# Eight transformer stages on one core: modulation pieces moved between stages, a new opening, forget gates by heads

## The chip, the cores and the metric

One core of one Trainium2 chip runs the whole program. The metric is the time of one execution on the device in microseconds, the median of three runs. Nothing is shared with another core; all tensors come from the chip's memory (HBM) and all are 32-bit floats.

## What is computed

256 tokens of width 1024 go through eight stages, in this order (the names are the kernel's): `moba` (attention of 8 heads, a pooled branch and two gates), `conv` (a gated feed-forward with a causal convolution of width 3), `ffn`, `swa` (attention of 16 query heads over a window), `ffn`, `ffn`, `fox` (attention of 16 heads with forget gates), `ffn`. Each stage is normalised, shifted and scaled, and added back through a gate:

```python
c_act = jax.nn.silu(c)
mod = c_act @ ada_w[l] + ada_b[l]          # (B, 6D) in the first block, (B, 9D) a layer in the second
h = rms_norm(x, norm_g) * (1 + scale) + shift
x = x + gate * mixer(h)                    # or 0.5 * gate * swiglu(h, w13, w2)

def swiglu(h, w13, w2):
    gate, up = jnp.split(h @ w13, 2, axis=-1)
    return (jax.nn.silu(gate) * up) @ w2

def fox_mixer(...):
    q, k, v, fl = jnp.split(h @ w_in, [HD, 2 * HD, 3 * HD], axis=-1)   # fl: one column a head, 16 in all
    log_f = jax.nn.log_sigmoid(fl + b_f)
    F = jnp.transpose(jnp.cumsum(log_f, axis=1), (0, 2, 1))            # over the 256 tokens
    s = q @ k.T + Fq[..., None] - F[:, :, None, :]
```

D is 1024, the hidden width of the feed-forwards 2816. `mod` holds shift, scale and gate of every stage: 6144 + 2 x 9216 columns, each a product of 1024 rows, which makes 48 chunks of 512 columns.

## The kernel before, in words

**Weight units.** Every weight matrix is cut into units of 128 x 2048 numbers (1 MB): 24 for `moba`, 33 for `conv` and each `ffn` (eleven steps `j` over 256 hidden columns, two units of the up projections and one of the down projection each, in the order `FFN_ORDER`), 10 for `swa`, 16 for `fox`. `W0[s]` is the first unit of stage `s`. The products keep 32-bit precision in three passes: a unit is split into a high part, `hi` (ACT, L504), and the rest, `lo` (DVE, `split_to`, L926), and so are the activations (`h_hi` and `h_lo`, `o_hi` and `o_lo`); PE does hi x hi, lo x hi and hi x lo into the same bank (lines in threes, such as L1411 to L1413 and L1374 to L1376). Raw units go through five slots that SP fills; slot w is free once PE is through with unit w - 5. `hi` and `lo` are double buffered. Each engine has its own list of work, written out by hand, and takes it strictly in order. `take(w)` on PE does what the schedule hangs onto unit w, and then waits for its `lo`.

**Modulation.** Four chunks of the 48 are done in the opening (`PRO_CHUNKS`), the others during the stages before the one that needs them: `CHUNKS_IN[s]` says how many in each. A chunk is four pieces of 256 rows by 512 columns (512 KB), loaded by POOL (L461) into the two halves of `ada`. Piece n can be loaded only when piece n - 2 has been used up. DVE adds a piece to one of two accumulators `ada_sum` in two steps (`ada_op`, L885 for a chunk's first step, L888 for the others), each a multiplication by the condition's column. When a chunk has its eight steps, PE sums it over the partitions (`sums`, L1342: four products of one column, eight records in the trace), DVE adds the bias (`columns`, L910) and for a gate's chunks PE turns the columns into rows (`gate_rows`, L1354). The first step of chunk c waits for the sums of chunk c - 2. `PIECES_AT`, `SUMS_AT`, `COLS_AT` and `GATES_AT` say behind or ahead of which unit each part stands. On DVE, the pieces of unit w come right after `lo` of unit w; on PE the sums of unit w come before its products.

The schedule of a `conv` or `ffn` stage before the change, for n0 chunks:

```python
at = [3 + (p0 * 27 // (4 * n0) if n0 > 4 else p0) for p0 in range(4 * n0)]
```

In the third stage (nine chunks) that is 36 pieces on units 3 to 29 with one or two each. In `swa`, unit 4 has two pieces and attention steps 8 to 15 one each; its three sums stand in step 1 and at its last units.

**Opening.** SP loads `c`, then five pieces of 512 rows by 512 columns (1 MB, rows of 2 KB), `x`, and three more pieces. DVE adds each with four steps of 512 columns (`pro_piece`), and PE sums each chunk as soon as it is there: two before the bias tables, two after the transposes of `x`. Then DVE makes `lo` of unit 0 and splits `h`.

**A stage's start.** `turn_x` on PE (L1362) turns the normalised `work` of 128 tokens (half t = 0 or 1), ACT applies shift and scale (L544), DVE splits (`split_h`, L961 and L963). DVE's `boundary` has the order: root of half 0, `lo` of unit 1, split of half 0, residual of half 1, `lo` of unit 2, root of half 1, `lo` of unit 3, split of half 1. ACT's has hi of unit 3 before `normed` of half 1 (L532).

**First stage's end.** DVE merges the two branches in four parts (semaphore `merged`), PE waits for all four, then `out_units` does four units for t = 0 and t = 1, with the gate rows due at the first.

**Forget gates.** 48 products (L1305 to L1307) with h as the weights and `f_hi` or `f_lo` of 16 columns moving give 128 tokens x 16 heads, twice. DVE adds the bias (L1263), ACT and DVE make log sigmoid, and PE adds up over the tokens with a triangular matrix (L1797 to L1799). Each token row is then 16 heads wide; `f_parts` holds the result by heads.

## Time and profile before

| what | value |
|---|---|
| three runs | 1540.94, 1527.5, 1535.44 us; median 1535.44 |
| the profiled execution | 1542.21 us, of which the span on the engines is 1540.4 |
| PE busy | 1454.9 us, 94% of the span |
| DVE, ACT, POOL busy | 1055.7 (69%), 732.5 (48%), 140.4 (9%) |
| mean granted clock of TensorE | 0.967 |
| moved by DMA | 333.94 MB, 217 GB/s on average |

The span is what the timeline shows; the profiled execution's time has 1.8 us around it and lies 0.4% above the median. PE's records overlap: a product's record is longer than the distance to the next, so its busy time is read as coverage, and the distance between starts is what a product costs.

### The profile page before, as it was taken

Reading aid. Unit: us, or ns where it says so; the run is one execution under the profiler, and the core shown is the slowest. Engines: PE = TensorE matmul, PEld = TensorE weight load, DVE = VectorE, ACT = ScalarE, POOL = GpSimd, SP = SyncE. Lnnn points to the kernel's source line nnn. Section 1 sums busy time; section 2 is a strip of 40 time slices with the busy share of each in tenths; the row PEclk is TensorE's granted clock in tenths of the full one; section 3 lists DMA queues with packets and bytes.
Section 4 is the critical chain, followed back from the end, with each engine's and each line's share of the span. In section 5 each row is a group of like instructions: output and inputs, shape, how many; then the busy total and the mean of one; then the engine's idle time right before and its main releaser. Section 6 shows DMA issues by size and latency. Waiting matters only on the chain.

```text
span 1540.4 us, 18813 instructions
## 1 busy us (share of the span) xinstructions
PE 1454.9 (94%) x7463; PEld 1208.0 (78%) x7463; DVE 1055.7 (69%) x1498; ACT 732.5 (48%) x1036; POOL 140.4 (9%) x199
## 2 busy tenths in 40 slices
PE   3799988999999999988999999999999899999998
PEld 2688978999978888765688878788877776688886
DVE  5768866988977777667577777776767346466444
ACT  2554445444564433765544335633337466554432
POOL 1011100110001111000011110011110100000000
PEclk9999999999999999985999999999999799999999
DMA  9677664777759888361478886788863442376552
GB/s 322 236 227 244 233 220 163 267 252 242 250 180 313 284 284 301 113 218 55 156 244 299 289 265 221 235 300 291 288 224 117 133 144 75 105 239 201 170 189 81
DMA packets 192395, 333.94 MB, mean 217 GB/s; under 512 B 8834, under 2 KB 132494, under 8 KB 192308
## 3 DMA queue, kind: packets, MB, share of 16 engines
q1 hardware_dynamic: 164464, 236.02, 45.6%
q0 software_dynamic: 27264, 96.49, 19.6%
q8 instruction: 60, 0.98, 0.3%
q10 hardware_dynamic: 580, 0.23, 0.1%
q14 instruction: 27, 0.22, 0.0%
HBM read 331.55 MB, written 1.15 MB: 216 GB/s over the span
## 4 chain that ended last, share of the span: by engine, by line
PE 67%; DVE 8%; ACT 5%; issue 3%; DMA 2%; ACTq 0%; DVEq 0%
PE bank L1411 9%; PE bank L1413 9%; PE bank L1412 9%; PE bank L1374 7%; PE bank L1376 6%; PE bank L1375 6%; DVE lo L926 3%; PE bank L1305 2%; PE bank L1307 2%; PE bank L1306 2%; PE bank L1539 2%; DMA ada<-in_ada_w 2%; DVE ada_sum L888 2%; PE bank L1342 2%; PE bank L1540 2%
## 5 line engine op out<-in xcount | busy, mean ns | idle before, releaser
L926 DVE TENSOR_TENSOR lo<-raw,hi 128x2048 fp32r<-128x2048 f32 x215 | 490.8, 2286 | 88.0 <-ACT hi L504 87.3
L504 ACT ACTIVATE hi<-raw 128x2048 fp32r<-128x2048 f32 x215 | 405.4, 1909 | 34.4 <-DMA raw<-in_w_out 13.9
L1411 PE MATMUL bank<-hi,h_hi 128*128 128x512 f32 x704 | 279.3, 397 | 2.6 <-DVE lo L926 1.8
L888 DVE SCALAR_TENSOR_TENSOR ada_sum<-ada,c_act,ada_sum 128x512 f32<-128x512 f32 x312 | 234.1, 750 | 65.2 <-DMA ada<-in_ada_w 56.7
L1413 PE MATMUL bank<-hi,h_lo 128*128 128x512 f32 x704 | 275.4, 391 | 0.0
L1412 PE MATMUL bank<-lo,h_hi 128*128 128x512 f32 x704 | 275.2, 391 | 0.0
L461 POOL DMA_DIRECT2D ada<-in_ada_w x176 | 125.3, 712 | 1105.8 <-DVE ada_sum L888 1090.4
L1374 PE MATMUL bank<-hi,o_hi 128*128 128x512 f32 x504 | 205.5, 408 | 8.6 <-DVE lo L926 7.6
L1376 PE MATMUL bank<-hi,o_lo 128*128 128x512 f32 x504 | 197.9, 393 | 0.0
L1375 PE MATMUL bank<-lo,o_hi 128*128 128x512 f32 x504 | 197.5, 392 | 0.0
L611 ACT ACTIVATE KT<-bank 128x256 f32<-128x256 f32 x88 | 33.8, 384 | 322.7 <-PE bank L1413 322.6
L1411 PEld LDWEIGHTS bank<-hi,h_hi 128*128 128x128 f32 x704 | 133.0, 189 | 32.6 <-DVE lo L926 3.5
L1413 PEld LDWEIGHTS bank<-hi,h_lo 128*128 128x128 f32 x704 | 132.8, 189 | 28.6
L1412 PEld LDWEIGHTS bank<-lo,h_hi 128*128 128x128 f32 x704 | 133.0, 189 | 26.5
L1305 PE MATMUL bank<-h_hi,hi 128*128 128x256 f32 x480 | 139.0, 290 | 1.0 <-DVE lo L926 1.0
L1306 PE MATMUL bank<-h_lo,hi 128*128 128x256 f32 x480 | 136.7, 285 | 0.0
L1307 PE MATMUL bank<-h_hi,lo 128*128 128x256 f32 x480 | 136.7, 285 | 0.0
L1374 PEld LDWEIGHTS bank<-hi,o_hi 128*128 128x128 f32 x504 | 95.4, 189 | 31.2 <-DVE lo L926 10.6
L1376 PEld LDWEIGHTS bank<-hi,o_lo 128*128 128x128 f32 x504 | 95.2, 189 | 21.2
L1375 PEld LDWEIGHTS bank<-lo,o_hi 128*128 128x128 f32 x504 | 95.7, 190 | 17.4
L1305 PEld LDWEIGHTS bank<-h_hi,hi 128*128 128x128 f32 x480 | 93.0, 194 | 3.0 <-issue 2.5
L1306 PEld LDWEIGHTS bank<-h_lo,hi 128*128 128x128 f32 x480 | 93.1, 194 | 0.2
(206 smaller groups left out, 1875.3 us busy)
## 6 DMA issues: line engine op xcount, KB each, us to landing
ada<-in_ada_w POOLq DMA_DIRECT2D x176, 512.0 KB, 5.3
raw<-in_ffn_w SPq DMA_DIRECT2D x176, 512.0 KB, 5.4
raw<-in_ffn_w SPq DMA_DIRECT2D x44, 1024.0 KB, 6.3
raw<-in_w_up SPq DMA_DIRECT2D x22, 1024.0 KB, 5.1
raw<-in_w_in SPq DMA_DIRECT2D x16, 1024.0 KB, 7.4
raw<-in_fox_w_in SPq DMA_DIRECT2D x12, 1024.0 KB, 5.1
raw<-in_w_down SPq DMA_DIRECT2D x11, 1024.0 KB, 5.2
raw<-in_swa_w_in SPq DMA_DIRECT2D x6, 1024.0 KB, 5.2
```

Of the source, the lines that this page charges most:

```text
L504: nc.scalar.activation(hi[:, n % NS, :], raw[:, n % NS, :], ACT.Copy).then_inc(hi_ready, 1)
L888: nc.vector.scalar_tensor_tensor(acc, in0=src, scalar=c_act[:, col:col + 1], in1=acc, op0=ALU.mult, op1=ALU.add).then_inc(ada_step, 1)
L926: nc.vector.tensor_tensor(lo[:, n % NS, :], raw[:, n % NS, :], hi[:, n % NS, :].bitcast(F32), ALU.subtract).then_inc(lo_ready, 1)
L1305: mm(outp, wh, xh, start=start, stop=False, skip_group_check=True)
L1306: mm(outp, wh, xl, start=False, stop=False, skip_group_check=True)
L1307: return mm(outp, wl, xh, start=False, stop=stop, skip_group_check=True)
L1374: mm(outp, xk_hi, wh[:, k, cut], start=start, stop=False, skip_group_check=True)
L1375: mm(outp, xk_hi, wl[:, k, cut], start=False, stop=False, skip_group_check=True)
L1376: ins = mm(outp, xk_lo, wh[:, k, cut], start=False, stop=stop, skip_group_check=True)
L1411: mm(bank[:, :], xk_hi, wh[:, i, :], start=k == 0, stop=False, skip_group_check=True)
L1412: mm(bank[:, :], xk_hi, wl[:, i, :], start=False, stop=False, skip_group_check=True)
L1413: ins = mm(bank[:, :], xk_lo, wh[:, i, :], start=False, stop=k == KD - 1, skip_group_check=True)
```

## The change

1. `CHUNKS_IN` goes from 6, 6, 9, 3, 9, 9, 0, 2 to 6, 7, 11, 0, 9, 9, 0, 2. `swa` (the fourth stage) has no pieces and sums any more. With more than ten chunks the schedule begins at unit 2, and a piece whose accumulator isn't free yet is put no earlier than the unit of that sum. In the third stage this gives, for units 2 to 27, the piece counts 2 2 2 1 2 2 1 2 2 0 3 1 2 2 2 2 1 2 2 1 2 0 3 1 3 1, with sums at units 5, 8, 12, 14, 16, 18, 20, 24, 26, 28 and 30.
2. Opening pieces are 128 rows by 2048 columns (rows of 8 KB), one step of 2048 columns each into one accumulator `pro_sum`; `x` is loaded fourth. All 16 sums of one column come after the last piece.
3. Forget gates: `f_hi` and `f_lo` are the weights, h moves (24 products of 256 columns), so that the result has a head in each row; DVE adds up over the tokens with a scan, and PE has no part in that.
4. First stage: columns a unit earlier; `out_units` waits for two merged parts before units 0 and 1 and for four before 2 and 3, and takes unit and gate rows first.
5. Start of `conv`: root and `normed` of half 1 come before `lo` of unit 2 and hi of unit 3, and PE turns half 1 only after both first units of half 0.

```diff
-CHUNKS_IN = [6, 6, 9, 3, 9, 9, 0, 2]
+CHUNKS_IN = [6, 7, 11, 0, 9, 9, 0, 2]
...
-        at = [3 + (p0 * 27 // (4 * n0) if n0 > 4 else p0) for p0 in range(4 * n0)]
-        for u0 in at:
-            PIECES_AT[w0 + u0] = PIECES_AT.get(w0 + u0, 0) + 1
+        from0, over = (2, 26) if n0 > 10 else (3, 27)
         turns, at_sums = [], []
-        for u1 in (at[4 * c0 + 3] + 2 for c0 in range(n0)):
+        for c0 in range(n0):
+            for p0 in range(4 * c0, 4 * c0 + 4):
+                u0 = from0 + (p0 * over // (4 * n0) if n0 > 4 else p0)
+                if c0 > 1:
+                    u0 = max(u0, at_sums[c0 - 2])
+                PIECES_AT[w0 + u0] = PIECES_AT.get(w0 + u0, 0) + 1
+            u1 = u0 + 2
...
-        COLS_AT.update({w0 + u: 1 for u in (11, 13, 15, 18, 20, 23)})
+        COLS_AT.update({w0 + u: 1 for u in (10, 12, 14, 17, 19, 22)})
...
-    elif kind0 == "swa":
-        PIECES_AT[w0 + 4] = 2
...
-            for i in range(8):
-                if i == 5:
+            for i in range(KD):
+                if i == 3:
                     sp.dma_start(x[:, :, :], a["x"][0].rearrange("(t p) d -> p t d", p=P)).then_inc(x_full, 16)
-                sp.dma_start(pro[i], ada_columns(i // 2)[:, 4 * (i % 2):4 * (i % 2) + 4, :]).then_inc(pro_full[i], 16)
+                sp.dma_start(pro[i], a["ada_w"][0][P * i:P * (i + 1), 0:2 * D]).then_inc(pro_full[i], 16)
...
                 split_to(W0[b] + 2)
                 norm_stats(b, 1)
-                split_to(W0[b] + 3)
-                normed(b, 1)
+                if KINDS[b] == "conv":
+                    normed(b, 1)
+                    split_to(W0[b] + 3)
+                else:
+                    split_to(W0[b] + 3)
+                    normed(b, 1)
...
             def pro_piece(i):
                 dve.wait_ge(pro_full[i], 16)
-                for k in range(4):
-                    ada_op(i // 2, 4 * (i % 2) + k, pro[i][:, k, :])
+                if i == 0:
+                    nc.vector.tensor_scalar(pro_sum[:, :], pro[i], c_act[:, 0:1], None, ALU.mult).then_inc(pro_step, 1)
+                else:
+                    dve.wait_ge(pro_step, i)
+                    nc.vector.scalar_tensor_tensor(pro_sum[:, :], in0=pro[i], scalar=c_act[:, i:i + 1],
+                                                   in1=pro_sum[:, :], op0=ALU.mult, op1=ALU.add).then_inc(pro_step, 1)
...
+                    nc.vector.tensor_tensor_scan(fz[:, 5, :], ones[0:16, 0:1].to_broadcast([16, T]), fz[:, 4, :], 0.0,
+                                                 ALU.mult, ALU.add).then_inc(cum_done, 1)
                     block_sums(s, 3)
                     block_norm(s, 3)
...
-                        if u:
-                            turn_x(s, 1)
+                    elif u == 0:
+                        turn_x(s, 1)
...
                 for o, t in [(0, 0), (0, 1), (1, 0), (2, 0), (3, 0), (1, 1), (2, 1), (3, 1)]:
                     if t == 0:
                         take(first + o)
+                        pe.wait_ge(merged, 2 if o < 2 else 4)
                     elif o == 3:
                         turn_x(s + 1, 0)
+                    if o == 0:
+                        pe.wait_ge((merge_a, merge_b)[t], 4)
...
-            sums(1)
             turn_x(0, 0)
             turn_x(0, 1)
-            sums(2)
+            pe.wait_ge(pro_step, KD)
+            for i in range(2 * KD):
+                ins = mm(M[:, i:i + 1], pro_sum[:, P * i:P * (i + 1)], ones[:, 0:1], start=True, stop=True)
+            ins.then_inc(ada_used, PRO_CHUNKS)
...
-                    pe.wait_ge(merged, 4)
                     out_units(s, h_hi, h_lo)
...
-                    for t in range(2):
-                        for k in range(KD):
-                            ins = product(A[0][:, 16 * t:16 * (t + 1)], h_hi[:, k, P * t:P * (t + 1)],
-                                          h_lo[:, k, P * t:P * (t + 1)], f_hi[:, k, :], f_lo[:, k, :], k == 0, k == KD - 1)
+                    pe.wait_ge(h_ready, 4 * s + 4)
+                    held = lambda w, k: w[:, k:k + KD, :].rearrange("p a b -> p (a b)")
+                    for k in range(KD):
+                        ins = product(A[0][:, 0:T], held(f_hi, k), held(f_lo, k), h_hi[:, k, :], h_lo[:, k, :],
+                                      k == 0, k == KD - 1)
                     ins.then_inc(fl_done, 1)
...
-                    pe.wait_ge(lf_ready, 1)
-                    lf = fz[:, 4, :]
-                    mm(A[1][0:16, 0:P], lf[:, 0:16], tri, start=True, stop=True)
-                    mm(A[1][0:16, P:T], lf[:, 0:16], ones[:, :], start=True, stop=False)
-                    mm(A[1][0:16, P:T], lf[:, 16:32], tri, start=False, stop=True).then_inc(cum_done, 1)
```

The diff also takes the calls of `columns`, `pieces` and `sums` out of `attention_step`, `step` and the `swa` branch, moves two small tables to other buffers and their waits with them, and puts `f_parts` before `lo` of unit 6 in `fox`.

## Rows read from the trace of the kernel before

**Rows 1.** The page's busy shares and granted clock in 40 slices.

```profile
PE 1454.9 (94%) x7463; PEld 1208.0 (78%) x7463; DVE 1055.7 (69%) x1498; ACT 732.5 (48%) x1036; POOL 140.4 (9%) x199
...
PEclk9999999999999999985999999999999799999999
```

**Rows 2.** The view of waits, PE: what line waited for what; us, times, longest us.

```profile
PE bank L1702 <- DMA TB<-in_fox_k_g: 17.3, 1, 17.3
PE bank L1362 <- ACT work L532: 8.7, 2, 4.4
PE bank L1374 <- DVE lo L926: 7.6, 11, 1.6
...
PE bank L1342 <- DVE modc L910: 6.1, 2, 3.6
...
PE bank L1797 <- DVE fz L1269: 5.1, 1, 5.1
```

**Rows 3.** Timeline, first stage: start, us, engine line op [idle before, releaser].

```profile
149.30 1.84 PE L1342 MATMUL bank<-ones,ada_sum 128*128 128x1 f32 x8 [2.55 <-DVE modc L910]
...
202.38 4.49 DVE L926 TENSOR_TENSOR lo<-raw,hi 128x2048 fp32r<-128x2048 f32 x2
...
202.52 2.08 PE L1354 MATMUL bank<-kon,modc 128*128 128x128 f32 x8 [4.46 <-DVE h_lo L1149]
...
204.82 0.63 PE L1375 MATMUL bank<-lo,h_hi 128*128 128x512 f32 x1
...
211.13 0.95 PE L1342 MATMUL bank<-ones,ada_sum 128*128 128x1 f32 x8
```

**Rows 4.** Timeline, the sixth stage's gap of 1.79 us.

```profile
1138.43 1.47 PE L1342 MATMUL bank<-ones,ada_sum 128*128 128x1 f32 x8 [1.79 <-DVE KT L1009]
```

**Rows 5.** Timeline, opening.

```profile
37.35 3.11 DVE L888 SCALAR_TENSOR_TENSOR ada_sum<-ada,c_act,ada_sum 128x512 f32<-128x512 f32 x4
...
40.68 1.84 PE L1342 MATMUL bank<-ones,ada_sum 128*128 128x1 f32 x8 [3.59 <-DVE modc L910]
...
46.33 0.77 PE L1539 MATMUL bank<-hi,h_hi 128*128 128x512 f32 x1 [3.81 <-DVE h_lo L963]
```

**Rows 6.** Windows: us, busy of PE, PEld, DVE, ACT, POOL; PEclk, DMA share, GB/s.

```profile
38.00:40.00 2.00, 0.00 (x0) 0.00 (x0) 1.89 (x4) 1.76 (x1) 0.00 (x0) 1.00 1.05 392
674.00:724.00 50.00, 42.17 (x136) 24.68 (x135) 34.32 (x106) 35.15 (x84) 1.42 (x2) 0.58 0.22 70
```

**Rows 7.** Timeline, start of the conv stage.

```profile
234.12 1.89 ACT L504 ACTIVATE hi<-raw 128x2048 fp32r<-128x2048 f32 x1
...
236.77 1.94 PE L1362 MATMUL bank<-kon,work 128*128 128x128 f32 x8 [4.42 <-ACT work L532]
...
238.26 0.48 DVE L885 TENSOR_SCALAR ada_sum<-ada,c_act 128x512 f32<-128x512 f32 x1
```

**Rows 8.** Timeline, forget gates of the seventh stage.

```profile
1193.89 0.17 PE L1305 MATMUL bank<-f_hi,h_hi 128*128 128x16 f32 x1
...
1201.21 0.77 PE L1539 MATMUL bank<-hi,h_hi 128*128 128x512 f32 x1
...
1215.67 0.60 PE L1797 MATMUL bank<-kon,fz 128*16 128x128 f32 x2 [5.06 <-DVE fz L1269]
```

**Rows 9.** Timeline, second feed-forward (third stage), a sum and the pieces behind it.

```profile
526.85 0.49 DVE L885 TENSOR_SCALAR ada_sum<-ada,c_act 128x512 f32<-128x512 f32 x1 [4.32 <-PE bank L1342]
...
528.42 0.70 POOL L461 DMA_DIRECT2D ada<-in_ada_w  x1 [7.74 <-DVE ada_sum L888]
...
529.68 2.28 DVE L926 TENSOR_TENSOR lo<-raw,hi 128x2048 fp32r<-128x2048 f32 x1
...
532.19 0.39 PE L1374 MATMUL bank<-hi,o_hi 128*128 128x512 f32 x1
...
532.66 1.54 DVE L888 SCALAR_TENSOR_TENSOR ada_sum<-ada,c_act,ada_sum 128x512 f32<-128x512 f32 x2 [0.69 <-DMA ada<-in_ada_w]
```

**Rows 10.** Tile ada from 440 to 620 us: DMA landing times.

```profile
DMA to landing us min/median/max: 4.1/5.3/8.1
```

More of the change, by code:

```diff
@@ L839, in _ @@
                     act.wait_ge(f_exp, 1)
[L840 removed]
+                    nc.scalar.activation(fz[:, 3, :], fz[:, 2, :], ACT.Ln, bias=ones[0:16, 0:1]).then_inc(f_ln, 1)
                     block_evict(s, 1)
@@ L971, in boundary @@
                 residual(b - 1, 1)
-                split_to(W0[b] + 2)
-                root(b, 1)
+                if KINDS[b] == "conv":
+                    root(b, 1)
+                    split_to(W0[b] + 2)
+                else:
+                    split_to(W0[b] + 2)
+                    root(b, 1)
                 split_to(W0[b] + 3)
@@ L1092, in attention_step @@
                     out_lo(s, (t - 3) // 2)
-                columns(int(t in COLS_STEP[kind]))
-                pieces(int(t in PIECES_STEP[kind]))
             def step(ins):
@@ L1168, in _ @@
                                     ALU.mult).then_inc(cols_done, 1)
-            columns(1)
-            pro_piece(4)
-            columns(1)
+            for i in range(4, 6):
+                pro_piece(i)
             root(0, 0)
             root(0, 1)
-            for i in range(5, 8):
+            for i in range(6, KD):
                 pro_piece(i)
-            columns(2)
+            dve.wait_ge(ada_used, PRO_CHUNKS)
+            nc.vector.tensor_tensor(modc[:, 0, 0:2 * KD], M[:, 0:2 * KD], cols[:, C_ADAB:C_ADAB + 2 * KD],
+                                    ALU.add).then_inc(mod_ready, PRO_CHUNKS)
+            dve.wait_ge(mod_ready, PRO_CHUNKS)
+            nc.vector.scalar_tensor_tensor(acol[:, 0, :], in0=modc[:, 0, KD:2 * KD], scalar=1.0,
+                                           in1=cols[:, C_N1:C_N1 + KD], op0=ALU.add, op1=ALU.mult).then_inc(acol_ready, 2)
             split_to(0)
```

80 lines of the change are left out of this document (35 added, 45 removed).

## The prediction

> **What bounds the kernel now.** I read the page's head first: PE is busy for 1454.9 of 1540.4 us and its granted clock is full in all but two of the 40 slices [rows 1]. So an edit pays only if it takes PE work away, closes one of PE's gaps, or spares the slow records that follow a gap. Then the waits of PE, longest first [rows 2]: of 85.5 us idle, 17.3 lie in the opening, where PE waits for first data and the change alters nothing; 8.7 are two stage boundaries (L1362), 7.6 are eleven short waits for a weight unit's low half (L1374), 6.1 are two sums held up by `modc` (L1342), 5.1 the forget gates (L1797); a sixth, of 4.5, ends the first stage (L1354, [rows 3]). The change aims at the last five. Last I read the timeline around each place, asking of each which engine arrives last and what stands before it in its order.
>
> **Full and half clock.** A 512-column product reads 0.63 us at half clock (1.2 GHz) and starts 0.43 after the one before; at full clock (2.4 GHz) it reads 0.39 (the row stands with the second feed-forward's) and starts 0.228 apart. The eight records of one sum read 0.95 at full clock and 1.84 at half [rows 3]. After a gap of 4.46 us PE goes on at half: gate columns and 24 products take 211.13 − 202.52 = 8.6 us, where 1.0 + 24 × 0.228 = 6.5 would do. I take 2.4 us of slow records behind each long gap. A gap of 1.79 us was enough once [rows 4].
>
> **Opening, +3.** Now the last piece is added in four steps of 0.78, 37.35 to 40.46, the last sum runs from 40.68 at half clock for 1.84, and the first product starts at 46.33 [rows 5]. The new pieces carry the same bytes in longer rows. The queue is already at 392 GB/s with a DMA share above 1 [rows 6], so they land no earlier: the last at about 35.5. One step of 2048 columns is bounded by the 2048-column `lo` subtraction, 4.49 for two [rows 3], and four of 0.78; I take 2.35, so DVE ends at 37.9, 2.6 us sooner. But three of the four groups of sums now run earlier, in PE's idle time; after the change all sixteen follow the last piece: 32 records of 0.23 at half clock, 7.4 us against 1.84, or +5.5. Net +2.9. At full clock they would take 3.8 and the part would be −0.6; since PE has been idle, I take half. Range −3 to +5, the lower end for pieces landing sooner.
> The Trainium skill (DMA: Bandwidth & Descriptors, "Why small descriptors are slow") puts a fixed overhead of about three cycles on each packet: from 2 KB to 8 KB rows that would be an estimated 3% of the landing time, about 0.7 us; the share above 1 in the row shows no room for it.
>
> **First stage inside, −1.5.** The columns are taken a unit earlier, which ends the wait of 2.55 us at 149.30 [rows 3] and the slow records behind it. DVE and the landings stand close behind, so I count half of the gap's 2.55 plus a little. Range −3 to 0.
>
> **Its end, −6.** Before `out_units` PE waits for all four merged parts: 4.46 us, then the gate columns 2.08 instead of 0.95 to 1.05 and the slow products, 1.4. Under the change the gate columns and the first two units need less and come first; the fourth part is ready about 4.4 us after PE's last product, and PE reaches it some 10 us on. All of 4.46 + 1.0 + 1.4 = 6.9 could go; that DVE also owes two `lo` of 2.28 each from 202.38 keeps me at −6.2. Range −7 to −5.
>
> **Conv's start, +3.** PE waits 4.42 us to 236.77 for the second half's `work`, turns it in 1.94 and goes on with u1 of the first half [rows 7]. Under the change u1 comes first and fills 2.9 of the gap. But ACT now makes `work` before hi(27), which moves from 234.12 to about 236 and ends 237.7; its `lo` ends 240.0; then come two pieces (2.9 us) where there was one (1.25, from 238.26), before the second half of `h` is split. That half is ready at 243.9 to 245.1, not 242.0, PE idles some 7.6 us in front of it and then runs at half clock: its first two units end at about 251.6, not 248.5. Range 0 to +4. The seventh chunk adds +0.5 in the body (0 to +1).
>
> **Second attention, −4.** Twelve pieces and three sums leave. At 674 to 724 us PE is busy 42.17 of 50 at a granted clock of 0.58, DVE only 34.32 [rows 6]: the steps there are short dependent ones, and DVE is not what they lack. What goes is DVE time ahead of waits at the edges: −3.9 (−2 to −8). The three sums cost 3.16 here and 3 × 0.95 where they go: −0.3.
>
> **Forget gates, −12.** Now 48 narrow products take 7.3 us (27 at 0.11 apart, the rest at 0.21, for PE falls to half clock amid them), and the twelve products behind them 5.5 instead of 2.7; a gap of 5.06 ends at 1215.67; three cumulative products take 1.4; the 24 products behind take 7.5 instead of 5.5 [rows 8]. After: 24 products of 256 columns at 0.12 are 2.9 (−4.4), the next twelve at full clock (−2.7), two waits for ACT's evictions of 0.9 and 1.5 in place of the gap (−2.6), no cumulative products (−1.4), no slow ones (−2.0): −13.1. I keep −12, range −14 to −8: a wait of 1.5 may bring half clock back. The scan is not in the trace; 256 columns lie between a 128x32 operation (0.19) and a 512-column one (0.75), and it stands on DVE beside 5 us of PE work: nothing.
>
> **The second feed-forward, +27.** This decides. Two chunks more come in: eight pieces, and the new schedule puts three pieces into one unit twice (u12, u24) and again at u26 with a `hidden` step; now none has more than two. `ada` has two buffers, so the third piece's load is issued only when the first has been used. One such cycle is in the trace [rows 9]. PE's sum lets DVE go at X = 526.85; the first piece is used up at X + 1.2; POOL issues its successor at X + 1.57; it has landed when DVE takes it at X + 5.8, after the `lo` of the next unit, which ended at X + 5.1, with PE needing it at X + 5.34: 0.2 us of slack. In the new unit the third piece stands ahead of that `lo`: it ends at X + 5.8 + 1.54 = 7.3, `lo` at X + 9.6, and PE stands still for 4.3 us. The whole wait lies on PE's path, since everything else on DVE's order is as late. So 4.3 at u12, 4.3 at u24, 5.0 at u26, and 1.1 for the step that turns the hidden units right behind. The start of the stage has pieces from its second unit now: two of them (2.9 us) stand ahead of the second half's root, and PE, which has no gap there now, gets 3.7 and then 1.5 of slow records: +5.1. Behind the three long stalls I add 2.4 each, 7.2. Sum 4.3 + 4.3 + 5.0 + 1.1 + 5.1 + 7.2 = 27. The load in the cycle took 4.24 from issue to landing; the stage's median is 5.3 [rows 10], and with it the sum is 33. If instead DVE catches up by way of gaps that I don't see, little of it comes: +3.
> The Trainium skill (DMA: Bandwidth & Descriptors, "Anatomy of one DMA — SWDGE (gpsimd) path") gives about 2.0 us plus the bytes over 436 GB/s for such a load, an estimated 3.2 us for 512 KB; the rows here never go below 4.1. By the page each stall would be 1 us shorter and this part an estimated +24.
>
> **Sum.** +3 − 1.5 − 6.2 + 3.1 + 0.5 − 3.9 − 0.3 − 12 + 27 = +9.7. The profiled execution took 1542.21, 6.8 above the median of the runs, 1535.44; its sum is 1551.9, and on the median that is 1545.
>
> **Rivals.** A, the feed-forward hides it: DVE is busy about 70% overall, and if it runs further ahead of PE at u12 and u24 than the 0.2 us above, the stalls shrink to 5 us in all. Then the gains stand almost alone: 1535 − 22 + 8 = 1521. For it: eleven waits for `lo` sum to only 7.6 us. Against: they exist at all, and slack in the cycle shown is 0.2. B, slower than before: loads of `ada` land in 6 to 8 us, since more of them run beside the weights; the stage shows up to 8.1 and 16.1 us of DVE waiting for them already [rows 10]. Each triple unit then costs 5.5 to 7 and units with two pieces also run late, about twelve of them by 0.5 each: +40 in the stage, 1558. It decides from a median landing of about 6. C, the forget gates give 5 rather than 12, because ACT's evictions hold PE and the clock stays at half: 1552. That the second attention loses nothing when its pieces leave, since it never waited for DVE, would be +4, within the range.
>
> **Chances.** The forecast 0.45 (own range 1536 to 1556), A 0.22 (1512 to 1526), B 0.22 (1554 to 1566), C 0.11 (1548 to 1556). The range 1519 to 1561 leaves out some 0.1 on either side. One per cent, about what a measurement of this kernel can tell from no change, puts the bounds at 1520.1 and 1550.8: faster 0.12 from A and a little from the forecast's edge, 0.15; slower is a quarter of the forecast, nearly all of B and two thirds of C, 0.39; the rest 0.46.
>
> **What would show it.** Right: in the second feed-forward three PE waits for `lo` of over 3 us, each with DVE waiting for `ada` just before; a DVE with 32 sum records of 7.4 us before the first product; no wait at L1354 at the first stage's end; the forget part from its first product to the first logits shorter by 12 us. Wrong: PE idle time in the second feed-forward up by under 8 us, or half clock absent behind the stalls; then I have mis-sized how far DVE runs ahead, and the change is a gain.

## Result: slower by 2.75%, and the profile after

The changed kernel takes 1576.08 us (median of 4 runs, 1572.44 to 1578.78) against 1533.2 for the kernel before (4 runs). The ratio is 1.0275, with a 95% interval of 1.0223 to 1.0327. The prediction said 1545, range 1519 to 1561. The profiled execution took 1578.78, its span is 1577.0; the terms of the prediction are compared with it.

The page's head and clock row (the counterpart of [rows 1]):

```profile
PE 1454.8 (92%) x7433; PEld 1202.7 (76%) x7433; DVE 1052.6 (67%) x1473; ACT 731.9 (46%) x1036; POOL 139.8 (9%) x198
...
PEclk9999998999999999898699999999999989999999
```

PE is busy exactly as long as before, 1454.8 against 1454.9 us. So whatever work the forget gates took from it, slow records elsewhere took again; all 36.6 us that the span grew are idle time of PE: 122.2 instead of 85.5. The view of waits says behind what (PE; us in total, times, longest; the counterpart of [rows 2]):

```profile
PE bank L1720 <- DMA TB<-in_fox_k_g: 26.4, 1, 26.4
PE bank L1394 <- DVE lo L933: 16.3, 12, 4.0
PE bank L1442 <- DVE KT L1020: 10.4, 5, 3.0
PE bank L1382 <- ACT work L536: 10.0, 3, 6.3
PE bank L1431 <- DVE lo L933: 6.7, 7, 4.4
...
PE bank L1326 <- DVE h_lo L970: 5.6, 1, 5.6
PE bank L1362 <- DVE o_lo L1244: 5.4, 1, 5.4
PE bank L1431 <- DVE h_lo L970: 4.9, 3, 4.4
...
PE bank L1603 <- DMA f_rows<-forget_rows: 2.2, 1, 2.2
```

L1720 is the old L1702, L1394 the old L1374. The three waits at which the change aimed (old L1342, L1354, L1797) are gone. In their place stand a longer first one, waits for `lo` twice as long in sum (26.6 us on all lines against 13.4), two waits that were short before (L1442 for `KT`, 1.6 on the old L1422, and L1431 for `h_lo`, 0.8 on the old L1411), and three that the trace before didn't have at all (L1326, L1362, L1603).

From the timelines of all kernels I made one table, which the rest rests on: the time of PE's first product, and then the length of each stage, from the start of its first `turn_x` on PE to the next stage's (for the first stage, from that first product).

| kernel | first product | moba | conv | ffn (3rd) | swa | ffn (5th) | ffn (6th) | fox | ffn | span |
|---|---|---|---|---|---|---|---|---|---|---|
| before | 46.3 | 179.4 | 207.4 | 199.8 | 129.9 | 202.4 | 205.2 | 169.6 | 200.3 | 1540.4 |
| after | 52.8 | 182.1 | 212.8 | 242.2 | 124.9 | 200.1 | 202.0 | 159.8 | 200.4 | 1577.0 |
| e1_old_schedule | 50.2 | 181.1 | 209.2 | 202.2 | 128.8 | 199.9 | 203.3 | 158.2 | 200.3 | 1533.3 |
| e2_four_buffers | 50.4 | 180.8 | 213.3 | 211.9 | 122.6 | 200.0 | 200.6 | 161.4 | 200.3 | 1541.2 |
| e3_table_later | 53.1 | 175.5 | 212.3 | 238.7 | 122.5 | 199.9 | 200.1 | 161.4 | 200.3 | 1563.8 |
| e4_short_rows | 47.7 | 180.5 | 213.2 | 242.4 | 122.6 | 199.9 | 204.1 | 161.4 | 200.3 | 1572.2 |
| e5_paced | 50.7 | 181.1 | 212.8 | 239.9 | 124.5 | 200.8 | 200.7 | 157.9 | 200.3 | 1568.6 |
| e6_old_boundary | 52.7 | 175.6 | 209.2 | 238.7 | 122.5 | 199.9 | 200.0 | 161.4 | 200.3 | 1560.3 |
| e7_piece_later | 52.8 | 180.9 | 213.4 | 240.8 | 124.5 | 200.3 | 202.6 | 156.6 | 200.3 | 1572.3 |
| e8_together | 46.4 | 175.8 | 209.5 | 204.0 | 130.0 | 199.9 | 202.0 | 161.3 | 200.3 | 1529.1 |
| e9_even | 50.2 | 182.1 | 213.1 | 228.8 | 122.5 | 201.5 | 203.2 | 158.2 | 200.3 | 1560.0 |
| e10_best | 44.8 | 176.0 | 208.8 | 204.1 | 125.0 | 202.8 | 200.4 | 156.8 | 200.3 | 1519.0 |
| e11_chunks_alone | 46.0 | 179.7 | 208.8 | 238.3 | 125.0 | 205.0 | 202.5 | 162.8 | 200.4 | 1568.4 |
| e12_gates_alone | 44.5 | 178.5 | 207.0 | 200.0 | 127.2 | 199.8 | 201.3 | 161.2 | 200.3 | 1519.9 |

The fifth and sixth stages have the same instructions in all of these and still vary by 5 us, so a difference of a few us in one stage of one trace is no finding by itself. The last stage varies by no more than 0.1.

**The opening.** Timeline of the kernel after (the counterpart of [rows 5]):

```profile
29.76 0.48 PE L1720 MATMUL bank<-kon,TB 128*128 128x128 f32 x1 [26.39 <-DMA TB<-in_fox_k_g]
...
31.61 0.17 DVE L1183 TENSOR_SCALAR cols<-cols 128x3 f32<-128x3 f32 x1 [6.79 <-ACT cols L722]
31.69 2.35 DVE L1177 SCALAR_TENSOR_TENSOR pro_sum<-V,c_act,pro_sum 128x2048 f32<-128x2048 f32 x1
...
41.83 1.44 PE L1733 MATMUL bank<-ones,pro_sum 128*128 128x1 f32 x6 [0.63 <-DVE pro_sum L1177]
...
52.78 0.76 PE L1559 MATMUL bank<-hi,h_hi 128*128 128x512 f32 x1 [3.97 <-DVE h_lo L970]
```

The large step takes 2.35, as estimated. But the small rows of biases and gains arrive for PE's L1720 at 29.8, not 20.5, and on DVE a small step on `cols`, which needs them, stands ahead of the fifth piece: DVE idles 6.79 us, and then four steps follow, each 2.35. The sums can start at 41.83 where the prediction had 37.9.

**The first stage's end and conv's start:**

```profile
212.37 1.15 POOL L449 DMA_DIRECT2D TB<-bias_by_distance  x1 [25.82 <-DVE h_lo L1158]
...
228.54 1.91 ACT L508 ACTIVATE hi<-raw 128x2048 fp32r<-128x2048 f32 x1 [13.84 <-DMA raw<-in_w_up]
...
234.85 1.97 PE L1382 MATMUL bank<-kon,work 128*128 128x128 f32 x8 [6.26 <-ACT work L536]
...
253.67 0.58 PE L1326 MATMUL bank<-hi,h_hi 128*128 128x256 f32 x1 [5.57 <-DVE h_lo L970]
```

At the sum of unit 18 PE is 9.6 us later than before (195.10 against 185.50); at the sum of unit 21, inside `out_units`, it is only 2.75 later (213.88 against 211.13). So a gain of 6.9 us at `out_units` is real. Then ACT waits 13.84 us for conv's second unit. And at 253.67 is the wait that the prediction had put at 7.6 us.

**The third stage.** The cycle of [rows 9], now at u12, where three pieces meet:

```profile
536.58 0.49 DVE L892 TENSOR_SCALAR ada_sum<-ada,c_act 128x512 f32<-128x512 f32 x1 [4.34 <-PE bank L1362]
...
538.16 0.71 POOL L465 DMA_DIRECT2D ada<-in_ada_w  x1 [10.83 <-DVE ada_sum L895]
...
542.18 1.54 DVE L895 SCALAR_TENSOR_TENSOR ada_sum<-ada,c_act,ada_sum 128x512 f32<-128x512 f32 x2 [2.68 <-DMA ada<-in_ada_w]
...
543.63 2.29 DVE L933 TENSOR_TENSOR lo<-raw,hi 128x2048 fp32r<-128x2048 f32 x1
...
545.98 0.80 PE L1394 MATMUL bank<-hi,o_hi 128*128 128x512 f32 x1 [3.90 <-DVE lo L933]
```

With X = 536.58 the third piece starts at X + 5.6 and `lo` ends at X + 9.3; the prediction had 5.8 and 9.6. What it didn't have is in the tile's view of the whole stage (DVE's idle time ahead of pieces, by what ended it; then landing times; the counterpart of [rows 10]):

```profile
  DMA ada<-in_ada_w: 36.4, 21
...
DMA to landing us min/median/max: 3.9/5.2/7.5
```

DVE waited 16.1 us for pieces in this stage before, 11 times. It is 36.4 now, 21 times, with the same landing times. So loads are not slower. There are more of them than two buffers let through without waits, where they stand.

### The profile page after: what moved, and what is told of

Its sections match the earlier page's. It is cut to its first block, busy times and chain, and to the rows that moved or that the text cites. A ratio compares the mean times of both kernels' runs of the same rounds, so it can differ in the third digit from the quotient of the medians.

```text
span 1577.0 us, 18727 instructions
## 1 busy us (share of the span) xinstructions
PE 1454.8 (92%) x7433; PEld 1202.7 (76%) x7433; DVE 1052.6 (67%) x1473; ACT 731.9 (46%) x1036; POOL 139.8 (9%) x198
## 3 DMA queue, kind: packets, MB, share of 16 engines
q1 hardware_dynamic: 161392, 236.02, 44.5%
## 4 chain that ended last, share of the span: by engine, by line
PE 70%; DVE 11%; DMA 9%; ACT 5%; issue 3%; ACTq 1%; POOL 0%; SPq 0%; DVEq 0%; POOLq 0%
PE bank L1431 8%; PE bank L1433 8%; PE bank L1432 8%; PE bank L1394 7%; DMA ada<-in_ada_w 7%; PE bank L1396 6%; PE bank L1395 6%; DVE lo L933 3%; PE bank L1326 3%; DVE ada_sum L895 3%; PE bank L1327 3%; PE bank L1328 3%; PE bank L1559 2%; PE bank L1561 2%; PE bank L1560 2%
## 5 line engine op out<-in xcount | busy, mean ns | idle before, releaser
L508 ACT ACTIVATE hi<-raw 128x2048 fp32r<-128x2048 f32 x215 | 405.5, 1909 | 44.8 <-DMA raw<-in_w_out 22.6
L1431 PE MATMUL bank<-hi,h_hi 128*128 128x512 f32 x704 | 280.6, 399 | 11.7 <-DVE lo L933 6.7
L1394 PE MATMUL bank<-hi,o_hi 128*128 128x512 f32 x504 | 208.0, 413 | 18.5 <-DVE lo L933 16.3
L1396 PE MATMUL bank<-hi,o_lo 128*128 128x512 f32 x504 | 200.1, 397 | 0.0
L1395 PE MATMUL bank<-lo,o_hi 128*128 128x512 f32 x504 | 199.8, 396 | 0.0
L1431 PEld LDWEIGHTS bank<-hi,h_hi 128*128 128x128 f32 x704 | 133.2, 189 | 43.1 <-DVE lo L933 10.0
L1326 PE MATMUL bank<-h_hi,hi 128*128 128x256 f32 x480 | 138.0, 288 | 1.0 <-DVE lo L933 1.0
L1394 PEld LDWEIGHTS bank<-hi,o_hi 128*128 128x128 f32 x504 | 96.7, 192 | 42.7 <-DVE lo L933 20.6
L1395 PEld LDWEIGHTS bank<-lo,o_hi 128*128 128x128 f32 x504 | 97.2, 193 | 17.8
L1326 PEld LDWEIGHTS bank<-h_hi,hi 128*128 128x128 f32 x480 | 91.9, 192 | 3.1 <-issue 2.5
```

The lines of the kernel that those rows point to most:

```text
L508: nc.scalar.activation(hi[:, n % NS, :], raw[:, n % NS, :], ACT.Copy).then_inc(hi_ready, 1)
L1326: mm(outp, wh, xh, start=start, stop=False, skip_group_check=True)
L1394: mm(outp, xk_hi, wh[:, k, cut], start=start, stop=False, skip_group_check=True)
L1395: mm(outp, xk_hi, wl[:, k, cut], start=False, stop=False, skip_group_check=True)
L1396: ins = mm(outp, xk_lo, wh[:, k, cut], start=False, stop=stop, skip_group_check=True)
L1431: mm(bank[:, :], xk_hi, wh[:, i, :], start=k == 0, stop=False, skip_group_check=True)
```

## Experiments

Ratios are against the kernel before, run on the same chip. The changed kernel's is 1.0275.

**1. The old schedule.** `CHUNKS_IN` back to 6, 6, 9, 3, 9, 9, 0, 2, with the old placing and the attention's pieces and sums; all other parts stay.

```diff
-CHUNKS_IN = [6, 7, 11, 0, 9, 9, 0, 2]
+CHUNKS_IN = [6, 6, 9, 3, 9, 9, 0, 2]
```

> The changed kernel with the old numbers of chunks (6, 6, 9, 3, 9, 9, 0, 2), the old placing of pieces and the pieces and sums back in the second attention; opening, forget gates, first stage's end and conv's start stay changed. Theory: the third stage's +42 us between the two traces come from its two added chunks, the conv body's +1.8 from its one, and the attention's gain of 6.3 from losing three. Then this kernel takes 1576 - 42 - 2 + 6 = 1538 (1534 to 1542), and the third stage has its old length of about 200 us. Rival: the third stage is slow because it starts later or with other states (loads, clock), not by its pieces; then it stays above 215 us and the kernel above 1550.

Measured: 1535.38, ratio 1.0008 (0.9976 to 1.0039). The third stage is at 202.2. So moving the three chunks costs all of the 2.7%, and the other four parts together gain nothing. Against the trace before, this one begins 3.9 us later and is 1.7 and 1.8 us longer in the first two stages, 7.4 together, which is about what the forget gates give when they stand alone (7.7, experiment 12).

**2. Four buffers for the third stage's pieces.** Two more in `V`, idle in that stage; 11 chunks and their placing unchanged.

```diff
+            b = i % 4 if s in WIDE else n % 2          # WIDE = (2,): the third stage
...
-                        pool.wait_ge(ada_step, 2 * (n - 1))
+                        pool.wait_ge(ada_step, 2 * (max(PREV[n], 0) + 1))
...
-                    pool.dma_start(ada[:, n % 2, :, :], ...
+                    pool.dma_start(pieces_of[BUF[n]], ...
```

> The changed kernel, with four buffers for the pieces of the third stage (two more in V, which that stage doesn't use) and nothing else altered. Theory A: two buffers bound the stream of pieces: a load of 5.2 us median plus 1.5 of use gives one piece in 3.5 us, where the schedule wants 44 in 26 units of 5.5. With four buffers DVE waits for ada under 5 us instead of 36, the three stalls of 4 us, the one of 4.4 at the start and the four before L1442 go, and the stage falls from 242 to 206 to 214: 1576 - 28 to - 36 = 1540 to 1548. Rival B: DVE's own work between two lo, three pieces of 1.5 us in one unit, is what is late: the stalls shrink by the third load's wait only, some 2.5 us each, and the kernel takes 1562 to 1570. Rival C: the DMA engines are the bound; then the landings grow to 8 us and more and little is won: over 1568.

Measured: 1544.65, ratio 1.0068 (1.0039 to 1.0096). The stage takes 211.9 instead of 242.2. The view of the tile has no wait for a DMA any more, and the three long stalls are left at 1.3, 1.3 and 1.9 us:

```profile
530.58 0.50 PE L1416 MATMUL bank<-hi,o_hi 128*128 128x512 f32 x1 [1.32 <-DVE lo L955]
...
606.54 0.50 PE L1416 MATMUL bank<-hi,o_hi 128*128 128x512 f32 x1 [1.32 <-DVE lo L955]
```

DVE does the same work in this stage and the DMA engines move the same bytes, so neither is what bound it: 30 of the 42 us were the two buffers.

**3. The table's load later.** POOL loads the second attention's table (2 MB) behind four of conv's pieces.

```diff
             pool.wait_ge(merged, 4)
+            load_pieces(1, 4)
             by_distance(1, 16)
```

> The changed kernel, with the load of the second attention's table of 2 MB issued behind four of the conv stage's pieces instead of ahead of them at the first stage's end. Theory: with out_units earlier, this load (issued at 212.4) now runs beside the load of conv's second unit (issued at 214.0, landed at 228.5), which ACT waits for; before it had run ahead of it. Moved, the unit lands in about 7 us, the gap of 6.26 us at 234.85 and the half clock behind it go: 1576 - 7 to - 9 = 1567 to 1569. Rival: the unit is late because its slot comes free late, or because the two pieces beside it are enough; then 1573 to 1577.

Measured: 1564.83, ratio 1.0192 (1.0128 to 1.0257). The first stage is 175.5 instead of 182.1, and ACT gets the unit at 221.73:

```profile
221.73 1.92 ACT L509 ACTIVATE hi<-raw 128x2048 fp32r<-128x2048 f32 x1 [6.93 <-DMA raw<-in_w_up]
...
246.79 0.58 PE L1327 MATMUL bank<-hi,h_hi 128*128 128x256 f32 x1 [7.37 <-DVE h_lo L971]
```

The gap of 6.26 is gone, as expected. The wait behind it grew from 5.57 to 7.37, now that nothing ahead hides part of it. 11 us were won in the median and 7 to 9 expected; of the 13.2 between the two traces, 6.6 lie in the first stage. The third stage (-3.5) and the attention (-2.4) are shorter too, but experiments 5 and 11 have a third stage about as short (239.9 and 238.3) and experiments 2, 4 and 9 the same attention (122.5 and 122.6) with the table where it was. So these two are not shown to come from the table.

**4. Opening pieces in short rows.** Each piece by four transfers of 128 x 512.

```diff
-                sp.dma_start(pro[i], a["ada_w"][0][P * i:P * (i + 1), 0:2 * D]).then_inc(pro_full[i], 16)
+                for g in range(4):
+                    sp.dma_start(pro[i][:, 512 * g:512 * (g + 1)],
+                                 a["ada_w"][0][P * i:P * (i + 1), 512 * g:512 * (g + 1)]).then_inc(pro_full[i], 16)
```

> The changed kernel, with each opening piece loaded by four transfers of 128 x 512, rows of 2 KB, into the same place. Theory: the small rows of biases and gains (580 packets on ACT's queue) take turns with the pieces' packets on each DMA engine, and a packet of 8 KB holds them four times as long as one of 2 KB: PE got them at 29.8 instead of 20.5, which held DVE's fifth piece to 31.7. With short rows they land at 20 to 23 again and the first product starts at about 49.5 instead of 52.8: 1573. Rival: they are late because of what is queued, not how long its packets are; then they land at 28 to 30 as well and nothing changes, 1576.

Measured: 1567.5, ratio 1.0207 (1.0130 to 1.0283).

```profile
17.71 0.47 PE L1722 MATMUL bank<-kon,TB 128*128 128x128 f32 x1 [14.46 <-DMA TB<-in_fox_k_g]
...
47.72 0.77 PE L1561 MATMUL bank<-hi,h_hi 128*128 128x512 f32 x1 [3.97 <-DVE h_lo L972]
```

1573 was expected, which its interval allows; between the two traces the difference is 4.8 us. The rows arrive at 17.7 instead of 29.8 and the first product comes 5.1 us earlier. But SP's issues spread out as well: with four times the packets its queue fills, and the last piece is issued after 22 us instead of at 6.5. So this run can't say whether it is the length of the packets or the depth of the queue.

**5. Long rows, paced.**

```diff
+                if i >= 3:
+                    sp.wait_ge(pro_full[i - 3], 16)
                 if i == 3:
                     sp.dma_start(x[:, :, :], ...
```

> The changed kernel, opening pieces with their rows of 8 KB, but SP issues piece i (from the fourth on, and x with it) only when piece i - 3 has landed, so that no more than three are queued. With rows of 2 KB (the run before) SP's queue was full and its issues spread to 25 us by themselves, so packet length and queue depth had changed together. Theory: packet length. There are still 8 KB packets in turn with the small ones, so the rows of biases and gains land at 26 to 30 us, the first product starts at 50 or later and the time is 1574 to 1578. Rival: depth of the queue. Then the rows land at 18 to 22 and the first product starts at 47.5 to 49, as with short rows: 1567 to 1570.

Measured: 1572.65, ratio 1.0263 (1.0234 to 1.0293).

```profile
24.84 0.33 SPq L413 DMA_DIRECT2D ada<-in_ada_w  x1
...
29.41 0.48 PE L1722 MATMUL bank<-kon,TB 128*128 128x128 f32 x1 [26.10 <-DMA TB<-in_fox_k_g]
```

The last piece is issued at 24.8, later than with short rows, and the small rows still arrive at 29.4. Experiment 4 issued late with short packets and had the rows early; this run issued late with long packets and had them late. So it is the length of the packets.

**6. The old order at conv's start**, on ACT, DVE and PE, in the kernel of experiment 3.

```diff
-                    elif u == 0:
-                        turn_x(s, 1)
+                        if u:
+                            turn_x(s, 1)
```

> The kernel with the table's load moved (1564.8), with the old order at conv's start on all three engines. Theory of the prediction: the new order costs about 3 us: in the kernel with the table moved PE stands still for 7.4 us before the second half's first unit, in the kernel before for 4.4 before its turn. So this kernel takes 1561 to 1563. Rival: the new order is no worse, since the two pieces behind lo(27) cost in the old order too (the seventh chunk brought the second one): 1564 to 1567.

Measured: 1562.17, ratio 1.0195 (1.0165 to 1.0224). By the ratio it can't be told from experiment 3. By the stage it can: conv takes 209.2 instead of 212.3, the 3.1 us of the prediction, and every other stage agrees with experiment 3 within 0.4 us. With six chunks the new order costs less, 209.2 (experiment 1) against 207.4. The second piece ahead of the split is the seventh chunk's, which would explain it; that is argued and not tried by itself.

**7. One piece of the first stage a little later.**

```diff
-        PIECES_AT.update({w0 + u: 1 + (u in (8, 9, 10, 11, 13, 15, 16, 17, 18)) for u in range(4, 19)})
+        PIECES_AT.update({w0 + u: 1 + (u in (8, 9, 10, 11, 13, 15, 17, 18)) for u in range(4, 20)})
```

> The changed kernel, with one of the two pieces behind unit 16 of the first stage moved on, so that units 15 to 19 have 2, 1, 2, 2, 1. Theory: earlier columns took away the wait at unit 12, but the pieces' stream through two buffers didn't get faster, so the wait came back at unit 17: PE idle 4.4 to 5.4 us at about 174, with DVE waiting 3.1 us for a piece ahead of o_hi and o_lo. One piece less ahead of them: that gap falls to 1.5 or less and the time by 3 to 5: 1571 to 1573. Rival: the gap hangs on something else ahead of o_lo (a late table or bank); then it stays above 4 and the time at 1576.

Measured: 1572.56, ratio 1.0258 (1.0232 to 1.0285). By the time this kernel can't be told from the changed one (1.0275, from 1.0223 to 1.0327), so the time supports nothing, and the mechanism fits only half. The gap that began at 174, 5.4 us, is down to 0.5, but one of 4.65 us stands at the next sum:

```profile
192.23 0.37 PE L1362 MATMUL bank<-ones,ada_sum 128*128 128x1 f32 x1 [4.65 <-DVE work L1143]
```

So the wait walks from the sum of unit 13 (2.55 before) to that of unit 16 (5.4 after) and on to that of unit 18. Moving one wait in this stage didn't remove any. `V` can't lend buffers here, since this stage uses it; more buffers were not tried in it.

**8. Three together**: experiments 1, 3 and 4.

> Old numbers of chunks, table's load behind four pieces, opening pieces with rows of 2 KB; forget gates, first stage's end, columns a unit earlier and the new conv order stay. If the three are independent, the measured differences add up: 1535.4 - 11.3 - 8.6 = 1515.5, faster than the kernel before by 1.2% (1513 to 1520). Rival: they overlap (a stage that starts earlier runs into the same load); then 1522 to 1528.

Measured: 1524.54, ratio 0.9954 (0.9930 to 0.9978). Faster than the kernel before, but 9 us short of the sum. That is no proof that the parts depend on each other: the interval of each of experiments 3 and 4 alone is 10 us or more to either side. What can be seen against experiment 1 is local and did add up: first product -3.8, first stage -5.3. The gains of experiment 3 in the third stage and the attention are not there (204.0 against 202.2, and 130.0 against 128.8).

**9. No unit with three pieces**, 44 pieces spread over units 2 to 29.

```diff
+EVEN_SUMS = [5, 8, 11, 14, 16, 18, 21, 24, 26, 28, 31]
...
-                if c0 > 1:
+                if n0 > 10:
+                    u0 = max(2 + p0 * 28 // 44, EVEN_SUMS[c0 - 2] if c0 > 1 else 0)
+                elif c0 > 1:
...
+            if n0 > 10:
+                u1, turns = EVEN_SUMS[c0], [12, 22]
```

> The changed kernel, with the 44 pieces of the third stage spread over units 2 to 29, none with more than two, and the sums and gate turns placed so that no piece waits for its accumulator. Theory: two things make the stage's +42, three pieces in a unit (stalls of 3.9, 4.0 and 4.4 us, each with about 2.4 of half clock behind it, 20 in all) and a stream through two buffers that is too slow for two pieces in a unit (the waits of 1.1 to 3.0 before L1442 and 4.4 at the start). The first goes, the second stays: DVE still waits 20 us or more for ada, the stage takes 218 to 226 instead of 242 and the kernel 1552 to 1560. Rival: the number of pieces alone sets it, however they are placed: the stage stays above 235 and the kernel above 1568.

Measured: 1554.92, ratio 1.0151 (1.0115 to 1.0187). The third stage takes 228.8, a little above the 218 to 226 of the theory and far below the rival's 235. DVE still waits for pieces:

```profile
  DMA ada<-in_ada_w: 31.0, 18
```

So both things are there: the placing is worth 13 us, and with this more even placing 44 pieces through two buffers still cost 29 against the 36 pieces before.

**10. The best version**: experiments 3, 4, 6, 9 and 2 together, with the new numbers of chunks.

> The changed kernel with everything that the runs so far point to: opening pieces in rows of 2 KB, the table's load behind four pieces, the old order at conv's start, the even placing and four buffers in the third stage. Stages by the runs so far: first product at 47, then 175.7, 209, 203 to 208, 122.5, 200, 202, 160 and 200: 1518 to 1524 in the profiled span, 1513 to 1521 as median, about 1% under the kernel before (1532). Rival: with no pieces in the attention and all of them at two a unit, DVE's own work bounds the third stage (four buffers left it at 212): then 1522 to 1528.

Measured: 1521.43, ratio 0.9925 (0.9901 to 0.9949). It beats both kernels, and lies at the upper edge of the 1513 to 1521 that I expected. The third stage holds its 44 pieces in 204.1 us, where 36 through two buffers took 199.8 to 204.0; the rival (DVE's work bounds it) falls. The view of waits of this kernel from 430 to 690 us has no wait of this stage above 1.1 us; the first line is the attention's:

```profile
PE bank L1620 <- DVE stat L1096: 5.7, 3, 3.2
PE bank L1453 <- DVE h_lo L996: 1.1, 1, 1.1
PE bank L1416 <- DVE lo L959: 1.0, 2, 0.7
```

**11. The chunks alone**, in the kernel before: its `CHUNKS_IN`, placing, and the attention's calls as in the change, nothing else.

```diff
-CHUNKS_IN = [6, 6, 9, 3, 9, 9, 0, 2]
+CHUNKS_IN = [6, 7, 11, 0, 9, 9, 0, 2]
```

> The kernel before with the new numbers of chunks and their placing alone. By the stages of the two traces: third stage +42, conv's body +2, attention -6: +38, 1570 (1566 to 1574). By the prediction's terms (+27 + 0.5 - 3.9 - 0.3) it would be +23, 1555. A rival that the other parts share in the third stage's loss (its start at another time against the weight loads) lies between, 1556 to 1565.

Measured: 1566.23, ratio 1.0215 (1.0178 to 1.0251), or +33. At the low edge of what I expected, above the prediction's +23. The third stage takes 238.3, 4 less than in the changed kernel. The seventh stage takes 162.8, with the forget gates as they were before.

**12. The forget gates alone**, in the kernel before.

```diff
+                    pe.wait_ge(h_ready, 4 * s + 4)
+                    held = lambda w, k: w[:, k:k + KD, :].rearrange("p a b -> p (a b)")
+                    for k in range(KD):
+                        ins = product(A[0][:, 0:T], held(f_hi, k), held(f_lo, k), h_hi[:, k, :], h_lo[:, k, :],
+                                      k == 0, k == KD - 1)
...
-                    pe.wait_ge(lf_ready, 1)
-                    lf = fz[:, 4, :]
-                    mm(A[1][0:16, 0:P], lf[:, 0:16], tri, start=True, stop=True)
```

> The kernel before with the new forget gates alone. The prediction said -12; the seventh stage shrank from 169.6 to 156.6 to 161.4 in the nine traces that have them, mean about -10. So 1521 to 1524 (ratio 0.993 to 0.995). Rival: part of that is chance of the phase in which the stage starts, and a new wait for the forget rows (2.0 to 2.2 us) grows when nothing else has changed: then -5, 1527.

Measured: 1524.71, ratio 0.9950 (0.9928 to 0.9973), or -7.7 us (-11 to -4). The seventh stage takes 161.2 instead of 169.6, but experiment 11 shows that the old gates can do with 162.8, so one pair of traces overstates the gain; the ratio is the better measure. A new wait shows where the first logits start:

```profile
1212.21 0.34 PE L1586 MATMUL bank<-KT,QT 64*128 64x128 f32 x1 [2.12 <-DMA f_rows<-forget_rows]
```

## Why the prediction was wrong

It said 1545 and the time is 1576. In the terms of its own sum, +9.7 against the profiled execution became +36.6, which is 27 us more. By the table, 15.4 of them lie in the third stage, 10.4 in the first, 3.5 in the opening, 2.2 in the forget gates' stage and 1.8 in conv. The second attention came out 0.8 below its term, and the fifth and sixth stages, which the change leaves alone, were 5.5 shorter. By stages:

**The third stage, +42.4 instead of +27: the step that failed most.** Everything the prediction worked out singly came true: 3.9, 4.0 and 4.4 us for the three stalls (said 4.3, 4.3, 5.0), 4.4 for the start (said 3.7 ahead of its slow records). What failed is the step that a stall comes only where three pieces meet. It took the load's cycle as a matter of single units and let all units with two pieces go free. But a piece occupies its buffer for the 0.3 until POOL issues, its load, 5.2 us in the median, and DVE's 1.5, 7.0 in all. A unit with two pieces right behind another one therefore needs some 7.0 us, and PE's products of a unit take 24 x 0.228, or 5.5. Units with one piece give time back, but few are left. How tight the whole is depends on what one takes for a unit: with the products alone, 25 units hold 39 pieces at one in 3.5 us, not 44; with the 6.05 us that a unit takes in the whole stage before (199.8 over 33), they hold 43. Both are estimates from these rows, and by both nothing is left over. I had this cycle in the price of the third piece and hadn't applied it to the other units. The rest came out at the places that "1.1 for the step that turns the hidden units" stood for: four waits before L1442, together 8.8. PE's gaps over 0.7 us in the stage sum to 26.7; two more sums are 1.9; what is left of 42.4, some 14, is slow records and short gaps, where I had counted 8.7. Experiments 2, 9 and 10 show it: buffers give back 30, placing 13, both 38 (in a kernel where the opening and conv's start had changed as well).

One sum and one reading of this part don't hold. With a load of 5.3 instead of 4.24 us three stalls become 1.1 longer each, which makes 30 and not the 33 that was said. And the granted clock was below full in three of the 40 slices [rows 1], not in two; nothing hangs on that.

**The first stage's end, -6, and conv's start, +3.** Both of these are right by themselves: `out_units` gives 6.9 us, and the new order costs 3.1 (experiment 6). The seventh chunk, +0.5 in the sum, costs about 1.4 in conv (208.8 in experiment 11 against 207.4). What failed is a step that wasn't made: what else hangs on `merged`. The wait on it stands on POOL too, ahead of the table's load of 2 MB and two pieces. Before, the table's load was issued at 202.8, 8.5 us ahead of the raw load of conv's second unit (211.3). Now `merged`, and with it the table's load, comes 9.6 us later, at 212.4. The raw load follows PE, whose units no longer wait for `merged`; it comes only 2.8 later, at 214.1, 1.7 us behind the table's, and shares the engines with 3 MB. It lands after 14.4 us instead of 7.4. Experiment 3 shows it, 6.6 us in that stage.

**First stage inside, -1.5.** The wait at the sum of unit 13 did go, but a larger one came at that of unit 16 (L1362, 5.4 us), where DVE had waited 3.1 us for a piece just before. With the table moved out of the way the stage is at 175.5, so all that the first stage's two edits gained is 3.9 us and not 7.7. That the wait goes from place to place is shown by experiment 7; that two buffers are its cause in this stage is argued by the same cycle and wasn't tried.

**The opening, +3.** It is +6.5 in the first product. 32 records of one column took 7.0 where 7.4 was said (and 4.4 to 7.0 in the other traces), so the term that I saw was about right. The term that I didn't see is the small rows, 9.2 us late, which moved DVE's end from 37.9 to 41.8. In the prediction "they land no earlier" was said of the pieces, and nobody asked what the pieces' packets do to others. Short rows (experiment 4) bring the first product to 47.7, and to 46.4 and 44.8 in experiments 8 and 10; the old opening has 46.3, 46.0 and 44.5 (before, experiments 11 and 12), so that the new one is worth about nothing.

**The forget gates, -12.** -9.8 in the trace, -7.7 as measured alone. The parts that I priced came as priced: the two waits for ACT's evictions were 0.9 and 1.1 (said 0.9 and 1.5), no gap, no cumulative products. By the prediction's own sign, from the first product of the gates to the first logits, it is 41.7 us before and 30.6 after, so 11.1 and not 12. One term is missing: with the products done earlier, PE reaches the logits before the forget rows have been written out and read back, 2.24 us of waiting at 1270.89. Behind it, in the ten us from 1275, the granted clock is 0.66; but the stretch from the first logits to the stage's end takes 101.4 to 104.5 us with the old gates and 102.8 to 107.5 with the new ones, so how much of that is due to the wait is open.

The nearness of 12 is in part luck. Some 7 of the 13.1 us were slow records in the trace before, where the 48 narrow products ran at a granted clock of 0.71. In experiment 11, with the same gates, they ran at 1.00 and took 5.2 us instead of 7.1, and the way to the first logits was 38.0: against that trace the new gates save 7.4. How slow the old ones run changes from trace to trace, and the prediction had one.

**The second attention, -4.** -5.0 in the trace after, and down to -7.4 in the others that have no pieces in this stage: inside the range. The four traces that have them vary from 127.2 to 130.0.

**The rivals.** A falls: PE's idle time in the third stage rose from 1.8 to 29.0 us. C falls for its reason: the two waits for ACT's evictions were 2.0 together, and the granted clock of the stretch was 1.00; but the gain alone, 7.7, lies nearer to its 5 than to 12. B (slower than before, 1558) had the right sign and the right place, but the wrong reason. It put +40 on the third stage, and the +42.4 there agrees by luck, since it needed landings above 6 us and they stayed at 5.2. Its remark that units with two pieces run late as well was the point, and that is so at the landing time that the trace before showed already. Its time, 1558, was still 18 too low. A page of the Trainium skill (DMA: Bandwidth & Descriptors, "Anatomy of one DMA — SWDGE (gpsimd) path") would give an estimated 3.2 us for such a load; the fastest in the third stage of the fourteen traces is 3.7 and the medians are 5.0 to 5.6, so the trace was the better source. The same page ("Why small descriptors are slow") lets one expect a little gain from long rows, and the opening lost by them. Another section of it, named below with the numbers, points at the cause.

## What to carry to other kernels

Where a stream runs through n buffers, divide first: load plus wait plus use, over n, times the number of pieces, against the length of the stage. Far below one, look only at single units; near one, as here, units that follow each other have to be looked at together. When a stall goes, list every queue that waits on the same event, and see what its transfers will now meet. And when transfers get larger packets, ask who takes turns with them.

## What the runs showed of the hardware

Small transfers that share the DMA engines with large ones are held by the length of the others' packets. ACT's queue carries 580 small packets in the opening, 36 for each of 16 engines. At the 392 GB/s of [rows 6] one engine moves 24.5 GB/s, so 2 KB take 0.08 us and 8 KB 0.33: if each small packet waits for one large one, that is 3 us or 12 us. The rows of biases and gains were there at 17.3 to 20.5 with opening rows of 2 KB (six traces) and at 29.2 to 30.1 with rows of 8 KB (eight traces), whether all nine megabytes were issued within 7.2 us (after) or at most four of them were under way (experiment 5).

The estimate differs by 9 us, the arrivals by 9 to 13. By the Trainium skill (DMA: Bandwidth & Descriptors, "Queues, rings and completion order") each DMA engine takes turns between the queues that it has work for, a whole packet at a time; a packet there is a group of some 9 to 17 descriptors, so the estimate above, which counts one row against one, is not worked out from the page. By this rule a small transfer waits for a packet of every other queue, however few are queued, and experiments 4 and 5 agree with it: shortening the rows helped, 17.7 against 29.8, and pacing them did not, 29.4.

Less work on PE didn't shorten its busy time in the changed kernel: 1454.8 us, as before, with the same 7433 instructions as in the best version, where it is 1437.0. The same instructions took 17.8 us longer. The best version has 82.0 us of idle time on PE against 122.2. Experiment 2 shows the link most closely, since it changes only the buffers of the third stage. Its windows of that stage, after and then experiment 2 (us, busy of PE, PEld, DVE, ACT, POOL; granted clock, DMA share, GB/s):

```profile
447.66:689.87 242.21, 213.21 (x958) 171.98 (x957) 161.14 (x188) 90.69 (x103) 31.25 (x44) 0.95 0.73 239
444.49:656.36 211.87, 202.35 (x957) 165.48 (x956) 161.29 (x188) 90.73 (x103) 29.93 (x42) 1.00 0.79 267
```

PE's idle time falls from 29.0 to 9.5 us, its busy time for the same instructions by 10.9, and the granted clock rises from 0.95 to 1.00. So of the 30 us that the buffers give back, about a third is not idle time but records that were slow.
